# Two transformer blocks on one Trainium2 core: the RWKV and dilated projections as three float32r passes, x kept in DRAM, and a pair's group norm output moved behind the next pair's level operands

## The reference, cut to what matters

```python
n = rmsnorm(h, norm_mix_g); proj = n @ w_in
# token shift on the RWKV part, then the split:
p_r, p_k, p_v, p_wd, p_ad, p_gd, q, k, v, gate_r, gate_a = split(...)
y_rwkv = rwkv7_mix(p_r, p_k, p_v, ...)        # 16 heads of 64, a recurrence over 512 tokens
yn = (y - mean) * rsqrt(var + GN_EPS) * gn_w + gn_b
y_rwkv = (yn + (sum(r * k * r_k) * v)) * g    # group norm output and bonus
y_attn = dilated_mixture(q, k, v)             # 12 heads, three dilations
merged = sigmoid(gate_r) * (y_rwkv @ p_rwkv) + sigmoid(gate_a) * (y_attn @ p_attn)
h = h + merged @ w_out
# memory cross attention, squared-relu feed forward, final norm
```

## Time and profile before

| | us |
|---|---|
| median of 3 runs (2767.25 to 2769.79) | 2769.64 |
| profiled execution, its own time | 2770.47 |
| its span, first to last instruction | 2768.7 |
| a pair pass (1644.11 to 1705.86) | 61.75 |
| pass 7 (1828.40 to 1889.20) | 60.80 |
| dilated attention (1889.20 to 2029.70) | 140.5 |
| eight pair passes from the first pass's projection (1394.4) | 494.8 |

### The profile page before, as it was taken

One profiled execution on the slowest core, in us unless ns is written; L12 is line 12 of the kernel. 1 busy time (PEld: TensorE's weight loads), 2 busy tenths in 40 slices (PEclk: granted clock), 3 DMA queues, 4 the chain that ended last, 5 costly groups with the idle time before them and its releaser, 6 DMA issues.

```text
span 2768.7 us, 43450 instructions
## 1 busy us (share of the span) xinstructions
PE 2689.2 (97%) x17783; PEld 1945.4 (70%) x17783; DVE 1662.4 (60%) x2208; ACT 656.2 (24%) x1147; POOL 202.4 (7%) x219
## 2 busy tenths in 40 slices
PE   7999899999999999999999999999989999999998
PEld 4545556888878878888655555574667888788887
DVE  4888766565466565554466666654465665655554
ACT  4234433111010121110233323322341211211102
POOL 2000321000000000000011111110000000100001
PEclk9999999999999999999999999999999999999999
DMA  7675203333323323333211111112123333233332
GB/s 263 196 249 188 77 24 102 95 93 100 97 82 99 97 85 91 98 95 97 78 42 42 35 35 35 35 58 73 37 59 97 93 112 102 69 99 99 98 92 76
DMA packets 394394, 255.54 MB, mean 92 GB/s; under 512 B 19767, under 2 KB 376720, under 8 KB 394128
## 3 DMA queue, kind: packets, MB, share of 16 engines
q1 hardware_dynamic: 391456, 246.78, 29.8%
q0 software_dynamic: 2320, 5.11, 0.6%
q10 hardware_dynamic: 480, 1.64, 0.2%
HBM read 250.61 MB, written 2.10 MB: 91 GB/s over the span
## 4 chain that ended last, share of the span: by engine, by line
PE 88%; DVE 7%; issue 2%; ACT 2%; DMA 1%; SPq 0%; DVEq 0%; ACTq 0%
PE PS L846 15%; PE PS L847 15%; PE PS L848 15%; PE PS L1675 5%; PE PS L1650 3%; PE PS L861 3%; PE PS L863 3%; PE PS L862 3%; DVE ARENA L2638 2%; PE PS L833 2%; PE PS L1764 1%; PE PS L1656 1%; PE PS L1358 1%; PE PS L1882 1%; PE PS L1538 1%
## 5 line engine op out<-in xcount | busy, mean ns | idle before, releaser
L872 DVE CAST WH<-W 128x1024 fp32r<-128x1024 f32 x304 | 213.3, 702 | 402.8 <-PE PS L848 359.1
L874 DVE TENSOR_TENSOR WL<-W,WH 128x1024 fp32r<-128x1024 f32 x304 | 374.6, 1232 | 10.4
L847 PE MATMUL PS<-XNL,WH 128*128 128x512 f32 x960 | 373.6, 389 | 0.0
L846 PE MATMUL PS<-HH,WH 128*128 128x512 f32 x672 | 262.0, 390 | 0.2 <-DVE HL L3023 0.2
L848 PE MATMUL PS<-HH,WL 128*128 128x512 f32 x672 | 261.5, 389 | 0.0
L847 PE MATMUL PS<-HL,WH 128*128 128x512 f32 x672 | 261.4, 389 | 0.0
L847 PEld LDWEIGHTS PS<-XNL,WH 128*128 128x128 f32 x960 | 180.2, 188 | 37.7 <-issue 0.7
L846 PE MATMUL PS<-XNH,WH 128*128 128x512 f32 x512 | 199.2, 389 | 0.0
L848 PE MATMUL PS<-XNH,WL 128*128 128x512 f32 x512 | 199.2, 389 | 0.0
L846 PE MATMUL PS<-XN2H,WH 128*128 128x512 f32 x448 | 176.9, 395 | 7.5 <-issue 7.5
L848 PE MATMUL PS<-XN2H,WL 128*128 128x512 f32 x448 | 174.5, 389 | 0.0
(11 more groups left out here) (520 smaller groups left out, 4640.3 us busy)
## 6 DMA issues: line engine op xcount, KB each, us to landing
ARENA<-in_ada_w SPq DMA_DIRECT2D x80, 512.0 KB, 5.2
W<-in_ffn_w SPq DMA_DIRECT2D x64, 512.0 KB, 3.8
W<-in_w_in SPq DMA_DIRECT2D x51, 512.0 KB, 4.5
W<-in_ffn_w_gate SPq DMA_DIRECT2D x44, 512.0 KB, 3.6
W<-in_ffn_w_up SPq DMA_DIRECT2D x44, 512.0 KB, 3.6
W<-in_ffn_w_down SPq DMA_DIRECT2D x32, 512.0 KB, 3.8
W<-in_sc_w_in SPq DMA_DIRECT2D x24, 512.0 KB, 3.7
ARENA<-in_ada_w SPq DMA_DIRECT2D x8, 1024.0 KB, 19.5
```

The source lines that it names most:

```text
L846: nc.tensor.matmul(dst, WH[:, h, c], hi(k), start=(start and k == 0), stop=False)
L847: nc.tensor.matmul(dst, WH[:, h, c], lo(k), start=False, stop=False)
L872: nc.vector.tensor_copy(WH[:, h, :], W[:, s, 0:D]).then_inc(parted, 1)
L874: nc.vector.tensor_tensor(WL[:, h, :], W[:, s, 0:D], WH[:, h, :], ALU.subtract).then_inc(freed[s], 1)
```

## The change

1. All products of `rw_first`, `rw` and `dil` become three float32r passes (`split_fill`). XN is split once: ACT rounds (XNH, in place of XR), DVE subtracts (XNL, in place of XN). Each weight unit is split by ACT (`weight_high`, a 128 x 1024 copy, or two of 128 x 512 where the buffer is B) and POOL (`weight_low`, the subtraction, over the unit's own slot). Per pass that is four of each. TensorE waits for the low part; ACT's copies of the high part stand between its other work (`hk` ahead of `raw0`, `hv` behind the transposes, `hd` behind `raw1`, `hr` behind `gg`); POOL does `lk` and `lv` ahead of the level masks, `ld` and `lr` behind them. `hr` waits for the next pass's first weights to land.
2. Token-wise units are gone: dilated units 6 to 8 are computed as the others, copied out, transposed by four matmuls (`value_turns`) and copied again.
3. x is written to DRAM behind the first block (POOL queue) and its SBUF tiles hold the RWKV output. Its squares and root are computed in the front; the root too is kept in DRAM, reloaded in dilated step 8 and inverted by DVE in step 12; x is reloaded (2 MB) behind the split of y and scaled by POOL during the merge.
4. DVE's order: a pair's 1/std stays first, but its three output operations and the bonus input go behind the level operands of the next pass (`zi`). Pass 0 is written out, passes 1 to 6 are the loop.
5. The merge runs gate_r, gate_a, p_rwkv, p_attn, with the gates on XNH and XNL, so XN is not split again. The wait ahead of a gate product on the sum of the iteration before stays as it was.
6. The dilated weights have one buffer pair instead of two.

```diff
+            def weight_low(slot, buf, p_act, high, p_pool, step, at=0):
+                pool.wait_ge(p_act.sem, p_act.done(high, at))
+                for own, high_part, low_part_ in weight_parts(slot, buf):
+                    ins = nc.gpsimd.tensor_tensor(low_part_, own, high_part, ALU.subtract)
...
             for i in range(RW_PAIRS - 1):
+                weight_low(ring.slot("rw", 1), "B", rw_act, "hk", rw_pool, "lk", i)
+                weight_low(ring.slot("rw", 2), "A", rw_act, "hv", rw_pool, "lv", i)
                 level_masks(i, i, rw_pe, rw_dve, rw_pool)
-                scaled(i)
+                weight_low(None, "B", rw_act, "hd", rw_pool, "ld", i)
+                weight_low(ring.slot("rw", 0), "A", rw_act, "hr", rw_pool, "lr", i)
...
+            def split_fill(slot, buf, ks, dst):
+                low = low_weights(slot)
+                for k in ks:
+                    h, c = k // 4, slice(k % 4 * P, (k % 4 + 1) * P)
+                    high = high_weights(buf, h)
+                    nc.tensor.matmul(dst, high[:, c], XNH[:, k, :], start=(k == 0), stop=False)
+                    nc.tensor.matmul(dst, high[:, c], XNL[:, k, :], start=False, stop=False)
+                    mm = nc.tensor.matmul(dst, low[:, h, c], XNH[:, k, :], start=False, stop=(k == KD - 1))
+                return mm
...
+            def weight_high(slot, buf, p_act, step):
+                for own, high_part, _ in weight_parts(slot, buf):
+                    ins = nc.scalar.activation(high_part, own, ACT.Copy)
+                ins.then_inc(p_act.sem, p_act.step(step))
...
+            for k in range(KD):
+                dve.wait_ge(norm_mix2.act.sem, norm_mix2.act.done(f"hi{k}"))
+                tt(XNL[:, k, :], XN[:, k, :], XNH[:, k, :], ALU.subtract)...
...
+            weight_low(ring.slot("rw_first", 0), "B", rf_act, "hr", rf_pool, "lr")
+            weight_low(ring.slot("rw_first", 1), "A", rf_act, "hk", rf_pool, "lk")
             for k in range(1, KD - 1):
...
+                nc.gpsimd.tensor_tensor(DIL0[:, 0, :], DIL0[:, 0, :], DIL0[:, k, :], ALU.add)...
...
                 tt(zs, zs, both("ident2"), ALU.add).then_inc(p_dve.sem, p_dve.step("zi"))
+                if ended:
+                    group_out(ended_at, signalled)
+                bonus_input(pair, p_dve)
...
-                stt(YC, YC, col("gn_w", i), RSTD[:, 0:T], ALU.mult, ALU.mult)...
-                stt(YC, YC, col("gn_b", i), BV, ALU.add, ALU.add)...
-                tt(y, YC, GG, ALU.mult).then_inc(p_dve.sem, p_dve.step("out"))
...
+            operands = ((xn_hi, xn_lo, KD, {}), (xn_hi, xn_lo, KD, {}),
+                        (lambda k: YRH[:, k, :], lambda k: YRL[:, k, :], KD, {0: "y3", 4: "y7"}),
+                        (lambda k: YAH[:, k, :], lambda k: YAL[:, k, :], 2, {0: "a1"}))
             with pe.Fori(0, KD) as i:
                 for u, (hi, lo, kts, parts) in enumerate(operands):
                     pe.wait_ge(mg_dve.sem, mg_dve.before("ra"[u % 2], i))
-                    split_product(pe, "merge", u, i, bank[u], hi, lo, kts,
+                    split_product(pe, "merge", u, i, bank[(u + 2) % 4], hi, lo, kts,
```

More of the change, by code:

```diff
@@ L577, in two_blocks @@
                             + next_pair("nmax ninv nk") + "bv gt0 gt1 dh st1 rq s1 s2 s3 s4 s5 s6" + next_pair("d2 m2") + "ys yc"
-                            + next_pair(front) + "grs yn yb out" + next_pair("rk"))
-            steps["pool"] = " ".join(f"m{l}0 m{l}1" for l in levels)
+                            + next_pair(front))
+            steps["pool"] = ("lk lv " if ahead else "l7 ") + " ".join(f"m{l}0 m{l}1" for l in levels) + (" ld lr" if ahead else " l1 l8")
         rw_pe, rw_act, rw_dve, rw_pool = (prog(f"rw_{e}", rw_steps[e], loop=True) for e in ("pe", "act", "dve", "pool"))
+        go_dve = prog("go_dve", "grs yn yb out", loop=True)
@@ L1025, in _ @@
                 nc.sync.dma_start(tiles(s), w_cols(w, AT_Q + 2 * P * u + P)).then_inc(landed[s], 16)
[L1026 to L1038, removed]
+            for i in range(KD):
+                for u, (weights, c0, kts) in enumerate(((w, GATE_R, KD), (w, GATE_A, KD), (a["p_rwkv_2"][0], 0, KD), (a["p_attn_2"][0], 0, 2))):
+                    s = ring.slot("merge", u)
+                    sp.wait_ge(freed[s], ring.free("merge", u, i))
+                    nc.sync.dma_start(tiles(s, kts), w_cols(weights, i * P + c0)).then_inc(landed[s], 16)
             with sp.Fori(0, 2) as i:
@@ L1670, in projection @@
+                def projection(u, ks, read, buf, low):
                     s = ring.slot("rw", u)
                     if ks[0] == 0:
-                        bank_read(read)
-                        pe.wait_ge(landed[s], ring.arrived("rw", u, i))
-                    for k in ks:
-                        mm = nc.tensor.matmul(bank[7], tiles(s)[:, k, :], xn(k), start=(k == 0), stop=(k == KD - 1))
+                        if u:
+                            pe.wait_ge(p_act.sem, p_act.done(read, at))
+                            pe.wait_ge(p_pool.sem, p_pool.done(low, at))
+                        else:
+                            pe.wait_ge(rw_act.sem, rw_act.before("dil", i))
+                            if i:
+                                pe.wait_ge(rw_pool.sem, rw_pool.done("lr", i - 1))
+                            else:
+                                pe.wait_ge(rf_pool.sem, rf_pool.done("l1"))
+                    mm = split_fill(s, buf, ks, bank[7])
@@ L1708, in pair_pass, with dilated @@
-                if ahead:
-                    projection(0, range(KD), "before")
-                else:
-                    dilated(7, range(KD), "before")
+                def dilated(u, ks, read, buf, low):
+                    if ks[0] == 0:
+                        pe.wait_ge(p_act.sem, p_act.done(read, at))
+                        pe.wait_ge(p_pool.sem, p_pool.done(low, at))
+                    mm = split_fill(None, buf, ks, bank[7])
+                    if ks[-1] == KD - 1:
+                        mm.then_inc(dw_used, 1)
@@ L1713, in pair_pass @@
+                if ahead:
+                    projection(0, range(KD), "dil", "A", "lr")
+                else:
+                    s = ring.slot("dil", 0)
+                    pe.wait_ge(rz_act.sem, rz_act.done("e6"))
+                    pe.wait_ge(rw_pool.sem, rw_pool.done("lr", RW_PAIRS - 2))
+                    split_fill(s, "A", range(KD), bank[7]).then_inc(freed[s], 1)
                 if i == 0:
@@ L1753, in pair_pass @@
                 if ahead:
-                    projection(1, range(0, 5), "raw0")
+                    projection(1, range(0, 5), "raw0", "B", "lk")
                 for l in levels:
@@ L1768, in pair_pass @@
                     if l == 0 and ahead:
-                        projection(1, range(5, KD), "raw0")
+                        projection(1, range(5, KD), "raw0", "B", "lk")
                     if l:
@@ L1865, in pair_pass @@
                 nc.tensor.matmul(bank[1], PAIR_ONES, CSQ, start=True, stop=True).then_inc(p_pe.sem, p_pe.step("var"))
+                if i == 6:
+                    pe.wait_ge(p_act.sem, p_act.done("dil", at))
+                    value_turns(DIL0, 6).then_inc(rz_pe.sem, rz_pe.step("t6"))
+                elif not ahead:
+                    pe.wait_ge(p_act.sem, p_act.done("late", at))
+                    value_turns(DIL0, 8).then_inc(p_pe.sem, p_pe.step("t8"))
             for i in range(RW_PAIRS - 1):
```

424 lines of the change are left out of this document (277 added, 147 removed).

## The result

The changed kernel takes 2745.25 us (median of 4 runs, 2742.95 to 2747.72) against 2769.72 before: ratio 0.9907, 95% interval 0.9895 to 0.9919. The profiled execution took 2746.42 us with a span of 2744.6.

A forecast was written before the change was run, and what follows sets the result against it. The prediction took TensorE, busy 97% of the span, as the bound, with DVE close behind in places. Front +6.5, passes -26, pass 7 -0.5, dilated attention -9 and merge +4 gave -25: 2769.6 to 2745 us, range 2714 to 2768.

The forecast's parts named there:

- Pass 7: Last pass: level operands 3 us earlier, ACT's tables +1.6, output ahead of first sum +3; total -0.5 us (-4 to +3).
- Dilated attention: Dilated units: gross saving 10.8 us, some 2 lost on steps where softmax is next; total -9 us (-12 to -4).
- The products: Float32r tiles: 0.68 us each, saving 0.18 a tile, 5.7 us a pass, of which TensorE can use 5.2.
- net gain of 3.8 a pass: Loop passes: 5.2 us saved less 1.4 for late first level sum and mean; pass 0 3.2; seven passes -26.
- The price of a collision: DVE beside POOL: operations with two SBUF operands or none in PSUM slow to 1.62 us from about 0.68.
- The moved output: Passes: 3.1 us of DVE operations move into 4.9 idle us before the first level sum, which comes 1.0 late.
- The front: Before pair 0: scaling and subtractions beside POOL end near 1379, operands at 1410 instead of 1403.7; +6.5 us (-3 to +10).
- The merge: Merge: 2.36 us split wait goes, seven gate_r waits add 4.2, POOL's scaling and reload 2; together +4 (-3 to +9).
- TensorE gets nearly all: Rival, all changed stages: TensorE keeps nearly its full saving, passes 35 us, total 2719 (2710 to 2728); chance 20%.
- POOL holds DVE: Rival, passes: DVE waits for whole POOL subtractions, +5 us a pass, total about 2806 (a third near 2771); chance 20%.
- The clock: Rival, passes: TensorE falls to 0.50 once a pass, losing 3.5 us each, 25 in all, total 2770; chance 5%.
- the prediction's last sign: Passes: the prediction is wrong if TensorE's granted clock leaves 1.00 there.

## Why the prediction was right, and where it was not

**The sum** was 2745 for 2745.25, but not every term earned it. Pass 7 was wrong by 7.2 us, beyond its bounds (-4 to +3). Dilated attention (2.3 better), the front (1.3 better) and a 2.6 us drift of the parts that don't change made up for it. That they cancel to a quarter of a microsecond is luck, and so in part is the 26.1 for 26 of the passes (next paragraph).

**The products.** A float32r tile at 0.68 held. TensorE's busy time in a pass fell by 5.1 where I had 5.7. Of the net gain of 3.8 a pass: passes 1 to 6 take 57.95 on average (347.7 us in all), 3.9 less; pass 0 takes 59.0, 2.8 less where I had 3.2 (see the clock below). The first level sum is 0.5 late and not 1.0, the mean 0.3 on average and not 0.4, the state copy costs its 0.4. The price of a collision was the right mechanism with the wrong size at single places (I took 1.62 for any operation beside POOL; the shift of v takes from 0.69 to 2.0, by where in POOL's instruction it falls).

**The moved output.** I had reckoned it as three operations that go into DVE's idle 4.9 us and make the first level sum a little late. That held. What it saves I had not asked: left where it was, it costs 33 us. 12.6 of them go with POOL's subtractions being whole (`lv` first of all); the rest goes with three operations ahead of operands on which TensorE waits. Cut the other way, some 8 of the 33 are TensorE's lower clock behind that wait. The move is no tidying beside the float32r products; they depend on it.

**The front** was +6.5 by DVE's end near 1379, operands at 1410; measured 1377.4 and 1407.6, with the block begun 1.4 us earlier. The sums of squares were the main cause: in the run without them beside the scaling the transposes come 5.7 us earlier, more than the whole +5.2.

**Pass 7** failed at the step "single tiles save 2.5, eight transposes and their copies cost 1: -0.5". I counted what the new steps take and what stands ahead of ACT's tables, but not that ACT's rounding of unit 8 had come to stand behind `gg`, and POOL's subtraction behind the rounding, ahead of a product that TensorE wanted at once. For the loop I had said that each low part is ready 2 to 10 us ahead of its product; I took that over to pass 7, whose order on ACT is another. It cost 3.4 us of waiting and 3.7 of clock. The output ahead of the first sum, priced at 3 and a collision, cost 2.9. With the rounding moved, pass 7 takes 53.1 us, 0.4 less than before, which is the -0.5; but the terms as I wrote them (-3, +1.6, +3, -2.5, +1) add up to +0.1 ahead of the collision, so that agreement is luck too.

**Dilated attention** gave the gross 10.8 and a little: the 2 us that I gave to softmax were not taken.

**The merge** came out by its working: the 2.36 is gone, and the product of gate and sum adds 0.7 to each of the seven waits; the first of them is 3.3, where DVE meets POOL's scaling of x.

**The rivals.** "TensorE gets nearly all" fell in every stage but dilated attention: passes 0 to 6 gave 26.1 us where it had some 35, the front and the merge cost 5.2 and 3.9, and pass 7 cost 6.7. "POOL holds DVE" is a true mechanism: with the output at its old place POOL's long instructions cost 12.6 us, half of the whole gain. In the order as changed it decides at one operation a pass, 0.2 to 0.6 us. "The clock" is true as well: it took 3.7 us in pass 7, and some 8 of the 33 with the output at its old place, but nothing in passes 1 to 6 as changed, which ran at 1.00. Pass 0 did not: behind the wait of 5.9 us for the front the granted clock was 0.57 from 1404 to 1412, and the first sixteen transposes took 3.68 us instead of 1.97. Of the prediction's last sign (wrong if the clock leaves 1.00 in the passes) the loop stays clear; pass 0 (0.97) and pass 7 (0.86) don't.

## What to carry to other kernels

When work is given to POOL, list DVE's operations with two SBUF operands that can fall beside it: each may wait for the end of POOL's instruction, so put work on PSUM there, move POOL's work to where DVE waits anyway, or cut it into pieces. A single SBUF operand is no safeguard by itself (next section). When a preparing step is added ahead of a product, go through every copy of the loop body, the last pass too, and ask what the step stands behind on its own engine. An idle stretch of TensorE is to be priced with the slow stretch that follows it: here the clock doubled the price of 3.4 us of waiting.

## What was not expected of the hardware

DVE's operation with two SBUF operands ended 0.54 to 0.56 us after POOL's subtraction in all of these places, where it met one in the middle: the product into X in each of passes 1 to 6 with the output at its old place (2.64 or 2.65 us instead of 0.69), the shift of v in five passes of the changed kernel (0.94 to 2.00). That is a little less than its own length.

An operation with one SBUF tensor can be held too, as the prediction's "or none in PSUM" allows, though it had no row for it. In the front of the changed kernel DVE scales a tile by a column beside a low part; its like a moment later is alone:

```profile
1391.32 2.77 POOL L1169 TENSOR_TENSOR RWF<-W,RWF 128x1024 fp32r<-128x1024 f32 x1 [6.31 <-ACT RWF L2469]
...
1391.91 2.46 DVE L3245 TENSOR_SCALAR ARENA<-ARENA,COLS 128x512 f32<-128x512 f32 x1
...
1398.46 0.46 DVE L3261 TENSOR_SCALAR ARENA<-ARENA,COLS 128x512 f32<-128x512 f32 x1
```

2.46 instead of 0.46, on the chain to the transposes of pair 0. The rounding copy of a weight split in the merge took 1.72 beside POOL's scaling of x and 0.69 later. The reciprocal kept its 3.35 beside `lk`, as the prediction took it.

POOL pays too: six sums took 10.09 us beside DVE and 8.32 nearly alone. Four pieces of 128x256 took 3.70 and 4.21 where one subtraction of 128x1024 takes 2.37; how much of that is DVE and how much the four instructions themselves, no run shows.
